# Hymba encoder layer on one core: the filter network's last layer as three split products instead of plain fp32 ones

## The reference, cut to what matters

```python
def hyena_filters(L, w1, b1, w2, b2, w3, b3, w4, freq):
    ...
    a = jnp.sin(fr * (z @ w1.astype(F32) + b1.astype(F32)))
    a = jnp.sin(fr * (a @ w2.astype(F32) + b2.astype(F32)))
    a = jnp.sin(fr * (a @ w3.astype(F32) + b3.astype(F32)))
    h = a @ w4.astype(F32)                  # (512, 64) @ (64, 2 * 512)
    ...
    h = h.reshape(L, 2, D_HYENA) * decay[:, None, :]
    return h[:, 0], h[:, 1]                 # forward and backward filters
```

## Time and profile before

| | before |
|---|---|
| median of 3 runs | 966.01 us (965.61 to 966.21) |
| the profiled execution's own time | 965.81 us |
| its span, first to last instruction | 964.0 us |
| PE busy | 957.5 us, 99% |
| DVE busy | 690.3 us, 72% |
| ACT busy | 439.8 us, 46% |
| granted TensorE clock, mean | 1.000 |

### The profile page before, as it was taken

The page is one execution under the profiler, slowest core; times in us unless marked ns, Lnnn a source line. Parts: engine busy times, 40 slices in busy tenths (PEclk is TensorE's granted clock), DMA queues, the critical chain, the costliest instruction groups (busy, mean ns, idle before and its releaser), DMA issues.

```text
span 964.0 us, 15092 instructions
## 1 busy us (share of the span) xinstructions
PE 957.5 (99%) x5483; PEld 824.9 (86%) x5483; DVE 690.3 (72%) x1067; ACT 439.8 (46%) x699; POOL 88.1 (9%) x104
## 2 busy tenths in 40 slices
PE   9999999999999999999999999999999999999998
PEld 7889999999888887677777878889999999988887
DVE  6888897887744438868898755789897788742333
ACT  6445665546333233234454563446565554622222
POOL 0011121210111010000000000002112121010100
PEclk9999999999999999999999999999999999999999
DMA  6456767675433346121221332256777767333322
GB/s 225 146 143 176 194 169 197 170 188 157 132 94 98 99 130 236 66 87 49 82 85 45 119 112 89 93 146 156 187 192 172 203 165 191 100 104 99 92 67 88
DMA packets 55029, 128.67 MB, mean 133 GB/s; under 512 B 5954, under 2 KB 14287, under 8 KB 54724
## 3 DMA queue, kind: packets, MB, share of 16 engines
q1 hardware_dynamic: 44452, 107.31, 34.4%
q0 software_dynamic: 10384, 20.67, 12.2%
q10 hardware_dynamic: 144, 0.05, 0.0%
HBM read 123.78 MB, written 4.22 MB: 133 GB/s over the span
## 4 chain that ended last, share of the span: by engine, by line
PE 94%; DVE 3%; issue 1%; ACT 1%; DMA 0%; DVEq 0%; SPq 0%; ACTq 0%
PE bank L2165 14%; PE bank L2167 14%; PE bank L2166 14%; PE bank L2223 8%; PE bank L2222 8%; PE bank L2221 8%; PE bank L2213 7%; PE bank L2215 3%; PE bank L2662 1%; PE bank L2664 1%; PE bank L2663 1%; PE bank L2554 1%; PE bank L2308 1%; PE bank L2309 1%; PE bank L2310 1%
## 5 line engine op out<-in xcount | busy, mean ns | idle before, releaser
L1223 DVE TENSOR_TENSOR w_lo<-raw,w_hi 128x1024 fp32r<-128x1024 f32 (+1 forms) x94 | 113.2, 1205 | 110.2 <-ACT w_hi L634 109.9
L634 ACT CAST w_hi<-raw 128x1024 fp32r<-128x1024 f32 (+1 forms) x94 | 95.0, 1011 | 187.5 <-PE bank L2167 172.4
L2165 PE MATMUL bank<-x_hi,w_hi 128*128 128x512 f32 x320 | 128.5, 401 | 0.1
L2166 PE MATMUL bank<-h_lo,w_hi 128*128 128x512 f32 x330 | 128.4, 389 | 0.0
L2167 PE MATMUL bank<-x_hi,w_lo 128*128 128x512 f32 x320 | 124.8, 390 | 0.0
L2166 PE MATMUL bank<-x_lo,w_hi 128*128 128x512 f32 x320 | 124.7, 390 | 0.0
L2221 PE MATMUL bank<-xt_both,w_hi 128*128 128x256 f32 x408 | 115.7, 284 | 0.0
L2223 PE MATMUL bank<-xt_both,w_lo 128*128 128x256 f32 x408 | 115.6, 283 | 0.0
L2222 PE MATMUL bank<-xt_both,w_hi 128*128 128x256 f32 x408 | 115.4, 283 | 0.0
L2221 PEld LDWEIGHTS bank<-xt_both,w_hi 128*128 128x128 f32 x408 | 77.0, 189 | 0.1
L2223 PEld LDWEIGHTS bank<-xt_both,w_lo 128*128 128x128 f32 x408 | 77.0, 189 | 0.0
(11 more groups left out here) (382 smaller groups left out, 2135.7 us busy)
## 6 DMA issues: line engine op xcount, KB each, us to landing
raw<-in_ffn_w_down SPq DMA_DIRECT2D x32, 512.0 KB, 3.5
raw<-in_ffn_w_gate SPq DMA_DIRECT2D x25, 512.0 KB, 4.0
raw<-in_ffn_w_up SPq DMA_DIRECT2D x25, 512.0 KB, 4.9
raw<-in_w_in SPq DMA_DIRECT2D x24, 512.0 KB, 3.2
raw<-in_ffn_w_gate SPq DMA_DIRECT2D x34, 256.0 KB, 3.1
raw<-in_ffn_w_up SPq DMA_DIRECT2D x34, 256.0 KB, 3.1
raw<-in_ffn_w_down SPq DMA_DIRECT2D x16, 384.0 KB, 3.1
sums<-in_ffn_w_gate SPq DMA_DIRECT2D x17, 256.0 KB, 3.6
```

The costliest lines, as they stand in the source:

```text
L634: nc.scalar.copy(w_hi[:, half, 0:kb, :], raw[:, slot, 0:kb, :]).then_inc(w_hi_made, 1)
L1223: nc.vector.tensor_tensor(w_lo[:, half, 0:kb, :], raw[:, slot, 0:kb, :], w_hi[:, half, 0:kb, :].bitcast(F32), ALU.subtract).then_inc(w_spl ...
L2165: nc.tensor.matmul(dst, w_hi[:, half, k, :], hi, start=first and k == 0, stop=False)
L2166: nc.tensor.matmul(dst, w_hi[:, half, k, :], lo, start=False, stop=False)
```

## The change

`filters(t)` on PE no longer takes one fp32 product per half but three fp32r ones: `act_hi` by `w4_hi`, `act_hi` by `w4_lo`, `act_lo` by `w4_hi`, the halves in turn. The parts are made as follows.

- `act_hi` by ACT right behind the third sine, `act_lo` by DVE behind the next `split`, both in the down projections.
- `w4_hi` by ACT (`w4_high`) behind `tap(1)`, and `w4_lo` by DVE (`w4_low`) behind `taps(1)`.
- PE waits in front of `filters(0)` for `w4_lo` (`w4_split`) and for `act_lo` (`mlp_split`), where it waited for `w4_set` before.

Two semaphores go: the `lambdas` load now counts on `mlp_landed`, and inside DVE's `filters(0)` the chain semaphore takes the place of `filt_read`.

```diff
--- before.py
+++ after.py
@@ -229,6 +229,10 @@
         decay, _ = place("decay", [P, NT, S], at=attn_at)
         w4, _ = place("w4", [P, D_HY], at=att_o_at)
         w4_back, _ = place("w4_back", [P, D_HY], at=att_o_at + 4 * S)
+        w4_hi, _ = place("w4_hi", [P, D_HY], F32R, at=att_o_at + 4 * S)
+        w4_lo, _ = place("w4_lo", [P, D_HY], F32R, at=att_o_at)
+        act_hi, _ = place("act_hi", [P, S], F32R, at=mlp_k_at)
+        act_lo, _ = place("act_lo", [P, S], F32R, at=tmp2_at)
         bias_row, _ = place("bias_row", [1, D_HY], at=att_o_at + 8 * S)
         end_u, _ = place("end_u", [1, P], at=att_o_at + 12 * S)
         ksig, _ = place("ksig", [P, 4, S], at=attn_t_at)
@@ -279,8 +283,8 @@
         early_landed = [sem(f"early_landed{n}") for n in range(12)]
         early_hi, early_split = sem("early_hi"), sem("early_split")
         x_landed = [sem(f"x_landed{k}") for k in range(KD)]
-        ident_landed, cols_landed, mlp_landed, lam_landed, dft_landed, late_landed, filt_landed = (
-            sem(n) for n in ("ident_landed", "cols_landed", "mlp_landed", "lam_landed",
+        ident_landed, cols_landed, mlp_landed, dft_landed, late_landed, filt_landed = (
+            sem(n) for n in ("ident_landed", "cols_landed", "mlp_landed",
                              "dft_landed", "late_landed", "filt_landed"))
         pool_moved, stored = sem("pool_moved"), sem("stored")
         bias_landed = [sem(f"bias_landed{i}") for i in range(2)]
@@ -301,7 +305,8 @@
         vec_sum, vec_set, rel_made, rel_split = (
             sem(n) for n in ("vec_sum", "vec_set", "rel_made", "rel_split"))
         lam_dot, lam_exp = sem("lam_dot"), sem("lam_exp")
-        w4_set, filt_sum, filt_read, filt_set = sem("w4_set"), sem("filt_sum"), sem("filt_read"), sem("filt_set")
+        w4_set, w4_hi_made, w4_split, filt_sum, filt_set = (
+            sem(n) for n in ("w4_set", "w4_hi_made", "w4_split", "filt_sum", "filt_set"))
 
         resid_moved = sem("resid_moved")
         qk_hi_made, qk_split = sem("qk_hi_made"), sem("qk_split")
@@ -425,7 +430,7 @@
             def others():
 
                 sp.dma_start(z_t[:], a["c_z"]).then_inc(mlp_landed, 16)
-                sp.dma_start(lam_in[:].rearrange("p k d -> p (k d)"), a["lambdas"].to_broadcast([P, 4 * DK])).then_inc(lam_landed, 16)
+                sp.dma_start(lam_in[:].rearrange("p k d -> p (k d)"), a["lambdas"].to_broadcast([P, 4 * DK])).then_inc(mlp_landed, 16)
                 sp.dma_start(rel[:], a["rel_bias"]).then_inc(late_landed, 16)
 
             def tables():
@@ -672,13 +677,12 @@
             def mlp_sin(k):
                 act.wait_ge(mlp_arg, k + 1)
                 nc.scalar.activation(act3[:], mlp_u[:], ACT.Sin).then_inc(mlp_act, 1)
-                if k < 2:
-                    act.wait_ge(mlp_act, k + 1)
-                    nc.scalar.copy(mlp_hi[:], act3[:]).then_inc(mlp_hi_made, 1)
+                act.wait_ge(mlp_act, k + 1)
+                nc.scalar.copy((mlp_hi if k < 2 else act_hi)[:], act3[:]).then_inc(mlp_hi_made, 1)
 
             def mlp_highs():
                 act.wait_ge(s_used, 7 * G0[1])
-                act.wait_ge(mlp_landed, 16)
+                act.wait_ge(mlp_landed, 32)
                 act.wait_ge(pool_moved, 16)
                 nc.scalar.copy(mlp_hi[:], z_t[:]).then_inc(mlp_hi_made, 1)
                 nc.scalar.copy(mlp_wr[:], mlp_w[:]).then_inc(mlp_hi_made, 1)
@@ -977,6 +981,10 @@
                 nc.scalar.activation(dst, zpad[:, m - 3, 1:S + 1], ACT.Identity, bias=col("conv_b", 4 * (m - 3) + g),
                                      scale=col("conv_w", 12 + 4 * (m - 3) + g)).then_inc(tap_set, 1)
 
+            def w4_high():
+                act.wait_ge(w4_set, 2)
+                nc.scalar.copy(w4_hi[:], w4[:]).then_inc(w4_hi_made, 1)
+
             def kernel_even(k):
                 act.wait_ge(kern_sum, 2 * k + 1)
                 nc.scalar.copy(ksig[:, 2 * k + 1, :], bank[6][:]).then_inc(kern_even, 1)
@@ -1061,6 +1069,8 @@
             for n in range(8):
                 split(8, N_MIX + n + 2)
                 tap(n)
+                if n == 1:
+                    w4_high()
                 for k in ((), (), (), (), (0,), (1,), (), ())[n]:
                     kernel_even(k)
             split(8, N_MIX + 10)
@@ -1323,7 +1333,8 @@
             def mlp_low(k):
                 dve.wait_ge(mlp_hi_made, k + 2 if k else 1)
                 source = act3 if k else z_t
-                nc.vector.tensor_tensor(mlp_lo[:], source[:], mlp_hi[:].bitcast(F32), ALU.subtract).then_inc(mlp_split, 1)
+                lo, hi = (act_lo, act_hi) if k == 3 else (mlp_lo, mlp_hi)
+                nc.vector.tensor_tensor(lo[:], source[:], hi[:].bitcast(F32), ALU.subtract).then_inc(mlp_split, 1)
 
             def mlp_weights_low():
                 dve.wait_ge(mlp_hi_made, 2)
@@ -1624,7 +1635,7 @@
                     dve.wait_ge(vec_sum, k + 1)
                     nc.vector.tensor_scalar(vec[:, k * S:(k + 1) * S], bank[k][0:HEADS, :], DK ** 0.5, None,
                                             ALU.mult).then_inc(vec_set, 1)
-                dve.wait_ge(lam_landed, 16)
+                dve.wait_ge(mlp_landed, 32)
                 for k in range(2):
                     nc.vector.tensor_tensor_reduce(lam_in[:, 2 * k, :], lam_in[:, 2 * k, :], lam_in[:, 2 * k + 1, :], 1.0, 0.0,
                                                    ALU.mult, ALU.add, lam[:, k:k + 1]).then_inc(lam_dot, 1)
@@ -1646,7 +1657,7 @@
                             mlp_argument((4 * i + j) // 2)[c]()
                         if arguments and c == 0 and 4 * i + j in (2, 4, 6):
                             mlp_argument((4 * i + j) // 2 - 1)[3]()
-                        if arguments and c == 2 and 4 * i + j in (0, 2, 4):
+                        if arguments and c == 2 and 4 * i + j in (0, 2, 4, 6):
                             mlp_low((4 * i + j) // 2)
                             if (i, j) == (0, 0):
                                 mlp_weights_low()
@@ -1723,8 +1734,7 @@
                     ins.then_inc(filt_set, 1)
                     nc.vector.tensor_tensor(hsum[:, t, :], total, decay[:, t, :], ALU.mult).then_inc(filt_set, 1)
                 else:
-                    nc.vector.tensor_tensor(hsum[:, 0, :], total, decay[:, 0, :], ALU.mult).then_inc(filt_read, 1)
-                    dve.wait_ge(filt_read, 1)
+                    link(nc.vector.tensor_tensor(hsum[:, 0, :], total, decay[:, 0, :], ALU.mult))
                     first = hsum[0:1, 0, :]
                     link(nc.vector.tensor_tensor(first, first, hdiff[0:1, 0, :], ALU.add))
                     nc.vector.scalar_tensor_tensor(first, first, 0.5, bias_row[:], ALU.mult, ALU.add).then_inc(filt_set, 2)
@@ -1734,6 +1744,11 @@
                 dve.wait_ge(filt_landed, 16 * 7)
                 for rows, op in ((slice(0, FO), ALU.add), (slice(FO, P), ALU.subtract)):
                     nc.vector.tensor_tensor(w4[rows, :], w4[rows, :], w4_back[rows, :], op).then_inc(w4_set, 1)
+
+            def w4_low():
+
+                dve.wait_ge(w4_hi_made, 1)
+                nc.vector.tensor_tensor(w4_lo[:], w4[:], w4_hi[:].bitcast(F32), ALU.subtract).then_inc(w4_split, 1)
 
             def taps(n):
 
@@ -1955,6 +1970,8 @@
                 for t in ((), (), (0, 1), (2, 3), (), (), (), ())[n]:
                     filters(t)
                 taps(n)
+                if n == 1:
+                    w4_low()
                 if n in (4, 5):
                     kernel_parities(n - 4)
                 for k in ((), (), (), (), (0, 1), (2,), (3,), ())[n]:
@@ -2478,9 +2495,13 @@
                     pe.wait_ge(root_made, 2)
                 if t > 1:
                     pe.wait_ge(filt_set, 2 * (t - 1))
-                for k in range(2):
-                    half = slice(k * FO, (k + 1) * FO)
-                    nc.tensor.matmul(bank[4 + 2 * (t % 2) + k][:], act3[half, of_order(t)], w4[half, :], start=True, stop=True).then_inc(filt_sum, 1)
+                for part, (a_part, w_part) in enumerate(((act_hi, w4_hi), (act_hi, w4_lo), (act_lo, w4_hi))):
+                    for k in range(2):
+                        half = slice(k * FO, (k + 1) * FO)
+                        ins = nc.tensor.matmul(bank[4 + 2 * (t % 2) + k][:], a_part[half, of_order(t)], w_part[half, :],
+                                               start=part == 0, stop=part == 2)
+                        if part == 2:
+                            ins.then_inc(filt_sum, 1)
 
             def kernel_sums(k):
 
@@ -2691,7 +2712,8 @@
             sum_squares(1)
             project(1, between={KD // 2: lambda: spread_tokens(1)})
             project(2)
-            pe.wait_ge(w4_set, 2)
+            pe.wait_ge(w4_split, 1)
+            pe.wait_ge(mlp_split, 5)
             filters(0)
             filters(1)
             project(3)
```

## The result

The changed kernel takes **970.32 us** (969.58 to 971.76, 6 runs), beside 966.11 us (965.61 to 966.43, 6 runs) of the kernel before: a ratio of 1.0045 [1.0035, 1.0055], 4.2 us slower. Forecast were 968.8 us and a range of 967.4 to 970.5. The direction was right and the median lies inside the range, at its upper end. 1.5 us are missing from the forecast time, and 1.3 us from the forecast difference of 2.9, since the median of before has moved by 0.1 as well. The profiled execution after is the fastest of its six, 969.58 us with a mean granted clock of 0.999; the other five, 970.18 to 971.76 us, had 0.996 to 0.998. It therefore shows what the sum was about, and hides the rest.

The account below looks back on a forecast made before the run. PE was taken to bound the kernel, busy for 957.5 of 964.0 us. A wait of 3.6 us less 0.71 us saved in the products gave +2.9 us, so 968.8 us, range 967.4 to 970.5.

Parts of the forecast that it names:

- The products: filters(0) to filters(3) on PE: three fp32r products take less time than one fp32 product, saving 0.71 us (0.2 to 0.83).
- The twin in attention: two_scores issues the same twelve fp32r matmuls as two new filters, in 1.92 us, with the halves side by side.
- rival 3: New filters matmuls: halves do not run side by side, or strided loads bind each pair; 2.8 us more, 971.6, chance 0.04.
- The stride: filters(0) and filters(1) load act with a stride of 4, costing 0.12 us at the entry alone.
- The high bound of 0.6: Strided weight loads of filters(0) and filters(1): 0.6 us if each of the six pairs waits for its loads.
- The wait: In front of filters(0), PE waits for w4_lo, made by DVE behind taps(1): 3.6 us late (3.4 to 3.8).
- DVE's delay: DVE moves by 0.6 us for w4_low, but PE reaches filters(2) later than DVE frees the banks: no cost.
- The rest: act_hi and act_lo hide in idle time of the down projections; semaphores, lambdas load and DMA cost nothing.
- Rival 1: The delay is given back later, in PE's six waits for attn_t, 2.5 us in all: 966.3, chance 0.09.
- Rival 2: PE's clock falls to its lower level after the hole: 1.8 to 3.7 us more, 970.6 to 972.5, chance 0.09.
- the sign that the prediction named: For Rival 2: matmuls behind the hole 0.45 us apart, about twice their distance of 0.23 us.
- the forecast case: PE idle once for some 3.6 us before filters(0), products save 0.71, clock costs nothing: 968.8 us, chance 0.76.

Follow-up runs that it names:

- Kernel 7: kernel 6 with taps(1), taps(2) put off behind work PE asks for, filters(2), (3) read before the split at n = 3: 965.32 us, ratio 0.9992.
- 10: Changed kernel, then Kernel 7, with the four stationary blocks read without gaps instead of with strides: 972.03 us and 965.38 us, one run each.
- Kernel 3: Changed kernel with the plain fp32 products put back; parts still made and PE still waits for them: 971.73 us, ratio 1.0052.
- kernel 4: As Kernel 3 (parts made, fp32 products), but PE waits only for w4_set as before: 966.96 us, ratio 1.0007.
- 5: Changed kernel with sum_weights before the split at n = 1 and w4_low before the taps: 967.02 us, ratio 1.0005.
- kernel 6: 5 with sum_weights before project(1), w4_low right behind it, w4_high before tap(1), filters(0), (1) read before the split at n = 2: 966.36 us, ratio 1.0.
- 2: Kernel before with only the diff's two semaphore replacements: 966.16 us, ratio 0.9998.
- experiment 1: Changed kernel run again with no edit: 970.92 us, ratio 1.005.
- experiment 8: Changed kernel with w4_low earlier in DVE's list (short hole): 968.41 us, ratio 1.002; or later (long hole): 972.59 us, ratio 1.0068.
- experiment 9: Changed kernel with four extra products, their result overwritten, in front of PE's wait: 969.30 us, ratio 1.0035.

## Why the prediction was right, and where it fell short

- **The products.** Forecast 0.44 - 0.12 + 0.39 = 0.71 us. Kernel 7, where nothing else stands in the way, shows 0.32 + 0.38 = 0.70. The twin in attention was the right row: 1.93 against its 1.92 us. The halves run side by side, so rival 3 falls.
- **The stride.** Forecast 0.12 us, measured 0.13 (10). The high bound of 0.6 assumed that each pair waits for its loads. None does, though each load is longer than the 0.23 us between two pairs: the recorded duration of a load is not what it costs in a row of them. By the Trainium skill ("TensorE: Matmul & The Clock Gate", on LDWEIGHTS) the columns alone would set it. That doesn't fit the 0.33 against 0.19 us of these loads, and would be off by 0.13 us in the sum.
- **The wait.** Forecast: first start 3.6 us late, released by DVE's `w_lo`, directly behind the last of `taps(1)`. Measured: idle for 3.49 us, and a start 3.56 us later than before (376.67 - 372.69 = 3.98, less the 0.42). Kernel 3 shows the whole loss with the wait and no new product.
- **DVE's delay.** Forecast to cost nothing, and it costs nothing in the changed kernel. The reason that was given holds only as long as PE is late itself: kernel 4 has the same delay without the hole, and it costs 0.61 us in the trace, 0.75 us in the medians. The prediction didn't say what this cover is worth; it is the price of putting the wait right and leaving DVE's order as it is (5 and 6).
- **The rest.** `act_hi` starts at 332.5 and `act_lo` at 338.72 us, both where the engines were idle; the semaphores cost nothing (2). `kernel_sums(0)` starts at 391.25, with the 0.42 taken off 390.83, forecast 390.9.
- **Rival 1** (given back later), 0.09: it didn't happen. PE's waits for `attn_t` in the profile after are the same 2.5 us, six times, 0.6 at most. One argument against this rival misread its row: the six are not all within 0.3 us, as they average 0.4 and one has 0.6.

```profile
PEld bank L2575 <- ACT attn_t L1010: 2.5, 6, 0.6
```

- **Rival 2** (PE's clock falls), 0.09: this is **the step that failed**. The sum put the clock at nothing, and the median has 1.3 to 1.6 us on top of 2.9. In experiment 1 the sign that the prediction named was there: matmuls 0.43 us apart behind the hole. Of 11 executions of the changed kernel one has a mean clock of 0.999, at 969.58 us; seven have 0.998, six of them at 970.18 to 970.58 us and one at 971.42; three have 0.996, at 970.92 to 972.21. Two of the 11 are profiled, one without a fall (969.58) and one with it (970.92). For the other nine the fall is inferred from time and mean clock together; a mean of 0.998 occurs in the kernel before too (966.07 us). As far as that goes, the forecast case describes one execution in eleven.

My argument against this rival was the earlier trace rows: one idle microsecond at the span's start at a clock of 1.00. That is no row of the same kind. It is less than a third as long as the hole, it comes before PE has done anything, and the row only says which clock was granted then. I also wrote that nothing in the trace contains such an idle stretch. That is wrong: the kernel before ends with one. Its last matmul, and the windows of the stretch behind it, from the trace of before:

```profile
958.36 0.85 PE L2355 MATMUL bank<-ident,x_fin 128*128 128x128 f32 x6
```

```profile
962.00:963.00 1.00, 0.00 (x0) 0.00 (x0) 0.00 (x0) 0.00 (x0) 0.00 (x0) 1.00 0.96 376
963.00:964.00 1.00, 0.00 (x0) 0.00 (x0) 0.00 (x0) 0.00 (x0) 0.00 (x0) 0.85 0.06 18
964.00:965.00 1.00, 0.00 (x0) 0.00 (x0) 0.00 (x0) 0.00 (x0) 0.00 (x0) 0.50 0.00 0
```

PE's work ends at 959.21, and with PE idle the clock falls to its lower level at 963.7, 4.5 us later. That alone doesn't say what 3.6 us of idle time do, but it shows that the clock does fall in this very program while PE has nothing to do, and it shows no idle stretch of that length after which it stayed up. The same stretch ends the traces of all the kernels here, and the fall comes 1.7 us (kernel 6) to 4.8 us (kernel 7) behind the last matmul. It agrees with the sentence of the Trainium skill ("TensorE: Matmul & The Clock Gate", section "HAM oscillation") that the prediction cites. With a row and a sentence for it and no row of its kind against it, a chance of 0.09 was far too low. The price, 1.8 to 3.7 us, was of the right size for a full fall: 2.4 us in experiment 1, 1.6 in the profile of the short hole, where the clock is low for half as long.

The account: the kernel is slower by 4.2 us = 3.6 for the hole, less 0.7 for the products, and 1.3 left over. Kernel 7 measures the products, the profiles after and of kernels 1 and 3 the hole, and 1 the price of a fall in one execution. That the 1.3 are the clock, in the median, is what experiment 9 supports: with the hole filled and the path unchanged, 1.0 of them goes, and 0.3 stays unexplained. That the range held was luck. It went to the edge of rival 2, for no reason that the measurement bears out, and the median of the repeat, 970.92 us, lies outside it.

## What to carry to other kernels

On an engine that bounds the kernel, a new operand made on another engine costs by its place in that engine's list, not by its length: 0.68 us of work cost 3.6 us here, because 3 us of work without a deadline stood ahead of it. Moving it ahead isn't enough where the engine has a backlog; the next entries then become the wait (5, 6), until what nobody asks for is behind all that is asked for (7). And a hole in TensorE's work is to be priced with the clock in it: when in doubt, put work of no use into the hole and see whether the kernel gets faster.

## What was not expected of the hardware

- **A short hole can be enough, and it differs from one execution to the next.** With 1.9 us of idle TensorE five of ten executions have the longer time and the lower mean clock, with 3.5 us the mean stayed at 0.999 in one of eleven of the changed kernel and in one of four of kernel 3 (969.66 us), with 5.2 us in none of four. The same kernel so has two times, 1.9 us apart (967.3 and 969.2 us in the middle of each group, experiment 8). The clock needn't fall inside the hole: in the profile of the short one it did 1.3 us behind it, in that of kernel 3 0.8 us.
- **The page can't show it.** 6.8 us at half clock take 0.35% off the mean clock of the span; in experiment 1 a single one of its 40 slices stood at 8, and in that of the short hole none. The mean clock of an execution is no proof either, since it also holds the fall behind the last matmul: kernel 6 has 0.998 in its profile without any fall before that. Windows of 2 us show it, and so does the distance between two matmuls, 0.43 instead of 0.23 us.
- **Executions drift.** In the first profile after, each start is late by 0.42 us before PE gets to the changed place, and by another 0.5 us or so towards the end, in loops that the change doesn't touch; others, of the kernels in 1 and 7, show no such drift. Medians of the kernel before differ by up to 0.4 us from chip run to chip run. A saving of 0.7 us can be read from the two blocks in one trace, and hardly from the times.
